# The experts' second bias, moved from the expert units into the routing stage

## The reference, cut to what matters

```python
top_logit, top_idx = lax.top_k(logits, TOP_K)
gates = jax.nn.softmax(top_logit, axis=-1)
...
hu = xblk @ w1[e] + b1[e]
act = x_glu * jax.nn.sigmoid(SWIGLU_ALPHA * x_glu) * (x_lin + 1.0)
return act @ w2[e] + b2[e]
...
y = zeros.at[row_tok].add(yb * row_gate[:, None])
h_lat = h_lat + g2[:, None] * y
```

## Time and profile before

| | us |
|---|---|
| median of 3 runs | 2738.23 (2736.86 to 2741.65) |
| the profiled execution, from its first to its last instruction | 2736.2 |
| TensorE busy | 2587.9 (95%) |
| VectorE busy | 2045.3 (75%) |
| ScalarE busy | 1453.7 (53%) |
| GpSimd busy | 539.6 (20%) |

### The profile page before, as it was taken

One profiled execution on the slowest core, in us unless ns is written; L12 is line 12 of the kernel. 1 busy time (PEld: TensorE's weight loads), 2 busy tenths in 40 slices (PEclk: granted clock), 3 DMA queues, 4 the chain that ended last, 5 costly groups with the idle time before them and its releaser, 6 DMA issues.

```text
span 2736.2 us, 46067 instructions
## 1 busy us (share of the span) xinstructions
PE 2587.9 (95%) x16405; PEld 2212.7 (81%) x16406; DVE 2045.3 (75%) x2500; ACT 1453.7 (53%) x1639; POOL 539.6 (20%) x423
## 2 busy tenths in 40 slices
PE   7998987999896999999999999999999999999995
PEld 3896866777885888777887979899989897898885
DVE  5447888545765987999879787866686778978786
ACT  5446565214443765777557465544454546645554
POOL 0035565200023112121212111110121112111111
PEclk9999998999998999999999999999999999999998
DMA  7121011442333996999879697866586779968783
GB/s 289 39 88 44 22 42 57 173 152 93 109 92 127 386 364 229 365 360 359 287 260 362 235 313 258 283 208 209 190 301 206 247 249 314 344 209 296 261 309 133
DMA packets 274722, 606.26 MB, mean 222 GB/s; under 512 B 21788, under 2 KB 52932, under 8 KB 273520
## 3 DMA queue, kind: packets, MB, share of 16 engines
q1 hardware_dynamic: 254256, 561.62, 57.1%
q0 software_dynamic: 20384, 43.51, 6.9%
HBM read 582.09 MB, written 46.97 MB: 230 GB/s over the span
## 4 chain that ended last, share of the span: by engine, by line
PE 40%; issue 10%; DVE 8%; ACT 4%; DMA 4%; DVEq 1%; POOL 1%; ACTq 0%; POOLq 0%
PE e_acc L2488 7%; PE e_acc L2491 7%; PE e_acc L2489 7%; PE e_acc L2461 5%; PE e_acc L2463 5%; PE e_acc L2462 5%; DMA list_now<-lists 3%; DVE e_slot_r L2646 3%; ACT whi L2574 3%; PE e_tb L2430 1%; DVE yo L2733 1%; DVE e_glu L2709 1%; PE e_acc L2523 1%; DVE e_xlo L2655 1%; POOL sum L2388 1%
## 5 line engine op out<-in xcount | busy, mean ns | idle before, releaser
L2574 ACT ACTIVATE whi<-e_slot 128x2048 fp32r<-128x2048 f32 x296 | 561.0, 1913 | 393.7 <-PE e_acc L2491 327.0
L2646 DVE TENSOR_TENSOR e_slot_r<-e_slot,whi 128x2048 fp32r<-128x2048 f32 x296 | 674.6, 2286 | 106.3 <-ACT whi L2574 106.3
L2488 PE MATMUL e_acc<-e_xhi,whi 128*128 128x256 f32 x1664 | 398.8, 282 | 3.3 <-ACT e_xhi L2578 3.3
L2574 ACT ACTIVATE whi<-slot 128x2048 fp32r<-128x2048 f32 x148 | 283.2, 1913 | 192.4 <-PE e_acc L2463 192.4
L2646 DVE TENSOR_TENSOR slot_r<-slot,whi 128x2048 fp32r<-128x2048 f32 x151 | 344.7, 2285 | 18.1 <-ACT whi L2574 16.5
L2461 PE MATMUL e_acc<-whi,e_ahi 128*128 128x512 f32 x800 | 319.4, 399 | 0.0
L2488 PEld LDWEIGHTS e_acc<-e_xhi,whi 128*128 128x128 f32 x1664 | 313.1, 188 | 6.3 <-ACT e_xhi L2578 6.3
L2463 PE MATMUL e_acc<-whi,e_alo 128*128 128x512 f32 x800 | 313.4, 392 | 0.0
L2462 PE MATMUL e_acc<-e_slot_r,e_ahi 128*128 128x512 f32 x800 | 311.5, 389 | 0.0
L2388 POOL DMA_INDIRECT sum<-yo,e_idx_now x48 | 117.8, 2454 | 973.3 <-issue 518.9
L2461 PE MATMUL e_acc<-whi,e_xhi 128*128 128x512 f32 x768 | 303.6, 395 | 1.8 <-DVE e_slot_r L2646 1.6
(11 more groups left out here) (432 smaller groups left out, 5014.9 us busy)
## 6 DMA issues: line engine op xcount, KB each, us to landing
e_slot<-in_w SPq DMA_DIRECT2D x296, 1024.0 KB, 7.1
slot<-in_w SPq DMA_DIRECT2D x151, 1024.0 KB, 6.4
rv<-in_w_ada SPq DMA_DIRECT2D x32, 512.0 KB, 5.6
slot<-in_w_in SPq DMA_DIRECT2D x9, 1024.0 KB, 9.6
wa<-in_w_ada SPq DMA_DIRECT2D x8, 1024.0 KB, 17.1
slot<-in_w_in SPq DMA_DIRECT2D x12, 512.0 KB, 4.2
xt<-in_x SPq DMA_DIRECT2D x8, 512.0 KB, 14.7
slot<-in_w_out SPq DMA_DIRECT2D x4, 1024.0 KB, 13.9
```

Of the source, the lines that this page charges most:

```text
L2488: pe.matmul(out[:, c, :], whi[i % RING][:, w], xhi[:, kk, :], start=first, stop=False, skip_group_check=True)
L2574: act.activation(whi[i % RING][:], raw[i % PIECES][:], ACT.Copy).then_inc(S["whi_made"], 1)
L2646: v.tensor_tensor(wlo[i % PIECES][:], raw[i % PIECES][:], whi[i % RING][:].bitcast(F32), ALU.subtract).then_inc(S["wlo_made"], 1)
```

## The change

The sum of gate times b2 is formed once per tile in `route` and added to the rows that are stored to `sum`. In `experts` the products with `pick2` and its copy go, and the first product of `down(8)` starts the accumulation.

In `route`, the b2 rows are loaded four times (32 rows each) into one tile, multiplied by g2 and split into high and low (`b2rows`). Per tile VectorE spreads the gates over the 32 experts, four times side by side (`gates_by_expert`), TensorE turns them (`turn_gates`), ScalarE and VectorE split them (`high_gates`, `low_gates`), TensorE multiplies them with `b2rows`, one product per half (`shared_rows`), and VectorE adds the halves to the residual rows, in place (`add_shared`). The store of a tile to `sum` moves behind that. The residual stays in the x tiles, now five; `hot` and `pick` are kept for two tiles and one tile instead of eight. The load of `b1rows` moves behind the load of the first weight pieces, and the last three tiles' shared rows come after it.

```diff
-        XS = 4
+        XS = 5
...
             for i in range(2, XS):
                 load(i)
+            for i in range(4):
+                sp.dma_start(vv[0][i * NE:(i + 1) * NE, :], dram["b2"][0]).then_inc(S["b2_in"], 16)
+            sp.dma_start(vv[1][:], dram["ada_rows"][:, 3 * D:].to_broadcast((P, D))).then_inc(S["b2_in"], 16)
...
             for i in range(LT):
-                sp.wait_ge(S["h_ready"], i + 1)
-                sp.dma_start(dram["sum"][i * P:(i + 1) * P, :], h_[i % 2][:]).then_inc(sum_out[i % 2], 16)
...
                 sp.wait_ge(S["v_ready"], i + 1)
                 sp.dma_start(dram["v_rows"][i * P:(i + 1) * P, :], vv[i % 2][:]).then_inc(v_out[i % 2], 16)
+                if 2 <= i < LT - 1:
+                    store_sum(i - 2)
+                    if i - 2 + XS < LT:
+                        load(i - 2 + XS)
             sp.wait_ge(S["y_done"], LT + 1)
             for i in range(SLOTS):
                 load_piece(sp, dram, keep, raw[i], i, slice(0, 1))
+            sp.wait_ge(S["h_ready"], LT)
+            sp.dma_start(b1rows, ...).then_inc(S["b1_in"], 16)
+            for i in range(LT - 3, LT):
+                store_sum(i)
...
+            def turn_gates(i):
+                pe.wait_ge(S["gates_ready"], i + 1)
+                pe.wait_ge(S["sum_ready"], i)
+                pe.transpose(pg, gates4[i % 2][:].rearrange("p g e -> p (g e)"), ident[:]).then_inc(S["gates_turned"], 1)
+
+            def shared_rows(i, n):
+                if n == 0:
+                    pe.wait_ge(S["gates_low"], 2 * i + 2)
...
+                pe.wait_ge(S["sum_part"], i)
+                pe.wait_ge(S["sum_ready"], i)
+                if n == 1:
+                    pe.wait_ge(S["sum_part"], i + 1)
+                pe.matmul(pb[:], gT[i % 2][:], b2rows[:, n * 512:(n + 1) * 512], start=True, stop=True).then_inc(S["shared_done"], 1)
...
             tt.then_inc(S["b1_turned"], 1)
+            shared_rows(LT - 3, 1)
+            turn_gates(LT - 2)
+            shared_rows(LT - 2, 0)
+            shared_rows(LT - 2, 1)
+            turn_gates(LT - 1)
+            shared_rows(LT - 1, 0)
+            shared_rows(LT - 1, 1)
...
+            act.wait_ge(S["b2_scaled"], 1)
+            act.activation(b2rows[:], vv[0][:], ACT.Copy).then_inc(S["b2_high"], 1)
+
+            def high_gates(i):
+                act.wait_ge(S["gates_turned"], i + 1)
+                act.wait_ge(S["shared_done"], 2 * max(0, i - 1))
+                act.activation(gT[i % 2][:], pg, ACT.Copy).then_inc(S["gates_high"], 1)
...
             exponents(LT - 1)
+            high_gates(LT - 2)
+            high_gates(LT - 1)
             act.wait_ge(S["y_done"], LT + 1)
...
+            def gates_by_expert(i):
+                v.wait_ge(S["pairs_ready"], i + 1)
+                c.link(v.tensor_tensor(gated[:], hot[i % 2][:], pairs[:, i, :, 1].unsqueeze(2).to_broadcast((P, TOPK, NE)), ALU.mult))
+                c.link(v.tensor_reduce(gate_of[:], gated[:].rearrange("p k e -> p e k"), AX.X, ALU.add))
...
+                v.tensor_copy(gates4[i % 2][:], gate_of[:].unsqueeze(1).to_broadcast((P, 4, NE))).then_inc(S["gates_ready"], 1)
+
+            def low_gates(i):
+                v.wait_ge(S["gates_high"], i + 1)
+                for at in (NE, 3 * NE):
+                    v.tensor_tensor(gT[i % 2][at:at + NE], pg[at:at + NE], gT[i % 2][at:at + NE].bitcast(F32), ALU.subtract).then_inc(S["gates_low"], 1)
+
+            def add_shared(i, n):
+                at = slice(n * 512, (n + 1) * 512)
+                v.wait_ge(S["shared_done"], 2 * i + n + 1)
...
+                v.tensor_tensor(x[i % XS][:, at], pb[:], x[i % XS][:, at], ALU.add).then_inc(S["sum_ready" if n else "sum_part"], 1)
...
                 if j == 0:
                     low_rows(0)
+            v.wait_ge(S["b2_in"], 16 * 5)
+            v.tensor_tensor(vv[0][:], vv[0][:], vv[1][:], ALU.mult).then_inc(S["b2_scaled"], 1)
+            v.wait_ge(S["b2_high"], 1)
+            v.wait_ge(S["b2_scaled"], 1)
+            v.tensor_tensor(b2rows[2 * NE:], vv[0][2 * NE:], b2rows[2 * NE:].bitcast(F32), ALU.subtract).then_inc(S["b2_ready"], 1)
             v.wait_ge(S["const_in"], 16 * NCONST)
...
                 if i:
                     residual(i - 1)
+                if i >= 3:
+                    low_gates(i - 3)
                 if i >= 2:
                     choose(i - 2)
                 if i + 1 < LT:
                     low_rows(i + 1)
+                if i >= 3:
+                    add_shared(i - 3, 0)
                 if i:
                     normed(i - 1)
                 if i >= 2:
                     targets(i - 2)
+                    gates_by_expert(i - 2)
+                if i >= 3:
+                    add_shared(i - 3, 1)
...
             v.wait_ge(S["units_done"], 2)
-            v.wait_ge(S["bias_ready"], 2)
+            for i in (LT - 2, LT - 1):
+                gates_by_expert(i)
+            for n in range(2):
+                add_shared(LT - 3, n)
+            for i in (LT - 2, LT - 1):
+                low_gates(i)
+                for n in range(2):
+                    add_shared(i, n)
+            v.wait_ge(S["bias_ready"], 1)
             v.wait_ge(S["b1_turned"], 1)
...
-                                if i == 8:
-                                    pe.matmul(out[:, b, :], pick2[:], bias[:, j * 512:(j + 1) * 512], start=True, stop=False)
...
-                    pe.wait_ge(S["pick_ready"], u * 2 + 2)
+                    pe.wait_ge(S["pick_ready"], u + 1)
...
-                v.tensor_copy(pick2[2 * NE:], own[2 * NE:, bass.ds(u, 1)].to_broadcast((2 * NE, P))).then_inc(S["pick_ready"], 1)
```

More of the change, by code:

```diff
@@ L1771, in route @@
         mlo = [t.sb(f"o_mlo{j}", [P, KT, P], F32R) for j in range(2)]
-        h_ = [t.sb(f"o_h{j}", [P, D]) for j in range(2)]
+        part = t.sb("o_part", [P, D])
         sq = t.sb("o_sq", [P, D])
@@ L1786, in route @@
         pairs = t.sb("o_pairs", [P, LT, TOPK, 2])
-        hot = t.sb("o_hot", [P, LT, TOPK, NE])
-        pick = t.sb("o_pick", [P, LT, TOPK, NE])
+        hot = [t.sb(f"o_hot{j}", [P, TOPK, NE]) for j in range(2)]
+        pick = t.sb("o_pick", [P, TOPK, NE])
+        gated = t.sb("o_gated", [P, TOPK, NE])
+        gate_of = t.sb("o_gate_of", [P, NE])
+        gates4 = [t.sb(f"o_gates4{j}", [P, 4, NE]) for j in range(2)]
+        gT = [t.sb(f"o_gT{j}", [P, P], F32R) for j in range(2)]
+        b2rows = t.sb("o_b2rows", [P, D], F32R)
         sel = t.sb("o_sel", [P, LT, NE])
@@ L1873, in project_out @@
                 for k in range(KT):
+                    if k in (2, 6) and i >= 3:
+                        shared_rows(i - 3, k // 4)
                     if k == KT // 2 and i >= 2:
@@ L1891, in project_last @@
                     for k in range(KT):
+                        if k == KT // 2:
+                            shared_rows(i - 3, n)
                         if (n, k) == (1, 0):
@@ L2007, in _ @@
                     turned_rows(i - 1)
+            high_gates(LT - 3)
             root(LT - 1)
@@ L2080, in targets @@
                 c.link(v.tensor_tensor(place[:, i, :], pp[:, i * NE:(i + 1) * NE], base[:], ALU.add))
-                c.link(v.tensor_tensor(pick[:, i], hot[:, i], place[:, i, :].unsqueeze(1).to_broadcast((P, TOPK, NE)), ALU.mult))
-                c.link(v.tensor_reduce(dest[:, four], pick[:, i], AX.X, ALU.add))
+                c.link(v.tensor_tensor(pick[:], hot[i % 2][:], place[:, i, :].unsqueeze(1).to_broadcast((P, TOPK, NE)), ALU.mult))
+                c.link(v.tensor_reduce(dest[:, four], pick[:], AX.X, ALU.add))
                 v.tensor_copy(desti[:, four], dest[:, four]).then_inc(S["dest_ready"], 1)
@@ L2125, in _ @@
             targets(LT - 2)
+            low_gates(LT - 3)
             choose(LT - 1)
@@ L2205, in shared @@
     keep["bias"] = top("bias", [P, 2 * D], F32R)
-    keep["pick"] = [top(f"pick{i}", [P, P], F32R) for i in (1, 2)]
+    keep["pick"] = top("pick", [P, P], F32R)
     keep["top"] = at
@@ L2458, in turn_act, with three @@
                         turn(lin[:, 0, :], 0, g % 2).then_inc(S["turned"], TURN_STEP[nb][g])
-                    def three(out, hi, lo, k, c, wh, wl, last):
-                        pe.matmul(out, hi[:, k, c], wh, start=False, stop=False)
+                    def three(out, hi, lo, k, c, wh, wl, last, first=False):
+                        pe.matmul(out, hi[:, k, c], wh, start=first, stop=False)
                         pe.matmul(out, hi[:, k, c], wl, start=False, stop=False)
@@ L2526, in down @@
                                     kk = 2 * (i - 8) + k
-                                    mm = three(out[:, b, :], ahi, alo, kk, slice(b * P, (b + 1) * P), whi[i % RING][:, w], wlo[i][:, w], kk == KT - 1)
+                                    mm = three(out[:, b, :], ahi, alo, kk, slice(b * P, (b + 1) * P), whi[i % RING][:, w], wlo[i][:, w], kk == KT - 1, kk == 0)
                             if j == 0 and between:
```

77 lines of the change are left out of this document (47 added, 30 removed).

## The result

The changed kernel takes 2749.59 us (median of 8 runs, 2742.33 to 2751.5), the kernel before 2737.9 in the same comparison (8 runs, 2732.91 to 2741.65): ratio 1.0039, interval 1.003 to 1.0048. That is 10.7 us more by the ratio; the medians are 11.7 apart. Predicted were 2740, range 2732 to 2748. The stages are read from one profiled execution of each kernel. That of the changed kernel took 2751.47 us, nearly the longest of its eight.

A forecast was written before the change was run, and what follows sets the result against it. TensorE was taken to bound large units and routing's tiles, VectorE small units. Terms -18.4 + 3.7 + 2.4 + 4.3 + 0.9 + 8.9 = +1.8 us gave a span of 2738.0, median about 2740, range 2732 to 2748.

The forecast's parts named there:

- The units: Experts' units: removed products save 12.0 us in large units, the dropped pick copy 6.0 in small ones; sum -18.4 us.
- C: Rival, faster: TensorE sets the small units, so 23 us goes, and the clock does not drop; 2733 us, chance 0.13.
- D: Rival: the removed products in the units were hidden and nothing goes; 2758 us, chance 0.02.
- These are queued behind a fifth x tile: Routing's start: b2 copies and gate row load behind an x tile, landing at 731.9 us, signal about 732.2.
- 3.7 us at turn 2: Routing's start: turn_merged(2) moves from 734.99 to about 738.7 us as VectorE waits for b2's loads; +3.7, bounds 3 and 5.
- The clock: Routing's start: after TensorE's 3.5 us pause it runs at 1.2 GHz for a while; +2.4 us, bounds 0 and 3.4.
- The tiles: Routing's tiles: ten added products and five gate transposes on TensorE, +4.3 us; VectorE's added work hidden; last tile +0.9.
- rival B: Slower: VectorE becomes the bound of routing's tiles, +5 us; 2745 us, chance 0.07.
- the worked-through tile: Routing: VectorE's steps in one tile end at 14.7 us, the next projection at 16.2, leaving 1.5 to spare.
- its extra chain of 0.9: Last routing tile: one product per half and ScalarE's high_gates ahead of root make it 0.9 us later, bounds 0.5 and 1.5.
- The end: Routing's end: b1's late landing, then a chain of products and additions across engines; +8.9 us, bounds 7 and 13.
- Rival A: Slower: handovers behind b1's landing make routing's end 13 us late, and its start pause reaches its bounds; 2746 us, chance 0.2.

The follow-up runs named there:

- e1: The kernel before without the units' b2 products and second pick copy, nothing put into routing (b2 missing from the output): 2719.66 us, ratio 0.9942.
- e3: The changed kernel with the four b2 loads and the gate row's load issued ahead of the router's weights, scaling left in place: 2741.51 us, ratio 1.0022.
- e12: e11 with 187 instructions of satisfied waits on TensorE, moving its loop over the units in the code without a branch: 2734.61 us, ratio 0.9993.
- e6: The kernel before with 35 never-executed products behind a branch, moving TensorE's loop over the units 72 instructions later: 2744.5 us, ratio 1.0028.
- e10: The changed kernel with VectorE's first subtraction of the experts' stage waiting until GpSimd has made both first gathers: 2743.98 us, ratio 1.0033.
- e7: The changed kernel with two small VectorE copies ahead of the first unit's pick, to start its subtractions later: 2747.97 us, ratio 1.0036.
- e2: The changed kernel with b2's scaling and split moved behind tile 0's residual and tile 2's low rows, loads unmoved: 2738.27 us, ratio 1.0007.
- e8: The changed kernel with b1 loaded earlier and the last shared products on free PSUM banks between the unit table's steps: 2738.75 us, ratio 1.0006.
- e4: The changed kernel with GpSimd's clearing of stale semaphores moved to the end of the experts' stage: 2749.51 us, ratio 1.0056.
- e11: The changed kernel with the edits of e2, e8 and e10 together: 2724.66 us, ratio 0.9955.

## Why the prediction was wrong

**The units: right.** -18.4 was said; e1 has -18.7 for units 1 to 36, and the changed kernel -17.1 without unit 4. TensorE's 0.23 us per product in large units and the pick in VectorE's unbroken row in small ones are borne out, so rivals C and D were rightly small.

No single step carries the miss. One term of the sum was mis-sized by much, and two costs were put at nothing.

**The failed step: "These are queued behind a fifth x tile", the landing at 732.2.** The product on b2 was to start there; it started at 738.95, 6.7 us later, of which 2.3 came from before routing. So 3.7 us at turn 2 became 8.1, and 6 to 11 over the seven profiles. Counted from the stage's first load, the row was forecast at 18.6 us and landed at 21.3 to 24.4. I divided the bytes in the queue by 353 GB/s and left out the two b1 loads issued right behind, which are under way beside the row. Their 0.52 MB are 1.5 us at that rate, an estimate. And the rate did not hold: 310 GB/s in 727.5 to 735.0 and 248 in 735.0 to 738.3, with DMA shares of 1.01 and 0.98. e3, with the same bytes earlier, takes 5.5 us back; how much of it is the b1 loads and how much the rate is argued, not shown. The operations' own chain was sized right: 6.5 us from product to turn, predicted and measured (738.95 to 745.41). The clock cost 1.6 instead of 2.4 (up to 2.4 in the other six).

**Two costs were put at nothing.** The larger is unit 4's stall, 4.5 us against e12's and e1's 40.3 to 40.4 (2.9 to 4.5 in the nine kernels of the new routing that have it), by 73 instructions of code put in ahead of the loop (e6 makes it in the old kernel, e12 removes it in the new one). The other is the first gather, 1.8 us: without the second pick it ends behind both of VectorE's subtractions instead of the first (e1 has it without any change to routing, e10 removes it). That VectorE's head start, 0.37 us larger by the dropped copy, is the reason was my guess, and e7 speaks against it: it gave the time back, and the gather still waited for both. Together the two are 6.3 of the 11.5 us by which the sum was short.

**The tiles: right in kind, too dear.** VectorE kept a wait of 1.80 us in each tile, so rival B was wrong and the worked-through tile right; a tile with two shared products and a turn of gates takes 16.18 us instead of 15.61, so products with several waits cost nearly their bare 0.23. The last tile took 1.0 more, so of its extra chain of 0.9 some 0.4 appeared. 2.8 instead of 5.2.

**The end: right mechanism, 1.6 short.** The chain ended 24.9 us after the last logits, as predicted (875.9 in the old clock is 24.8), by luck, two errors that cancel: it began 1.0 earlier, and product and addition took 1.67 instead of 1.4. Short were SyncE's last store, 3.3 us from issue to passing instead of 2.6, and the meeting of the engines behind it, 1.0 us, which I left out. Rival A names this relay, but its point, routing over 24 us longer, was not reached: 23.0 without what came before.

Of the 11.5 us between the forecast sum and the measured one, 3.6 are the start, 1.6 the end, 4.5 unit 4, 1.8 the gather and 2.3 scatter before routing; the tiles gave 2.4 back.

## What to carry to other kernels

A load is priced by when its row lands among everything under way on the same engines, with a range of some us for it, not by bytes over the best rate; and work that waits for it does not stand ahead of a row the tensor engine needs (e2: one move, 8.8 us). A relay between two engines over one PSUM bank costs its whole chain, here 1.67 us a link, so work appended at a stage's end is put on free banks between steps that already wait (e8: 9 us). And where the sum nearly cancels, look also at what merely shifts: an engine's code, and what runs beside a gather at the next stage's head. A stage is read in more than one execution before a few us of it are explained.

## What the runs showed of the hardware

**Code.** TensorE idled 3.0 to 3.4 us at the first small unit behind a large one in nine kernels (the changed one, e2 to e4 and e7 to e11) and in e6, with a 16 KB transfer on the instruction queue just ahead, and was granted a clock of 0.50 for 3.4 to 6.8 us from around its end on. It is a matter of the first passes: in the changed kernel the last such transfer began at 1098.8 us, and the loop ran 32 more times without one. The Trainium skill, "Runtime: NRT & Kernel Launch", Instruction fetch mechanics, says code comes in 16 KiB blocks of 256 instructions and a taken branch to a block not held must wait for its transfer. That would explain e6: the loop was moved by 72 instructions, 0.28 of a block. The trace agrees in the size of the transfer and in the stall at a branch; which block it was, no run shows.

**Gathers.** An indirect gather's instruction took 1.0 to 1.1 us where no 128x2048 subtraction of VectorE ended in it. All others, 73 or 74 of the 74 gathers in each of the fourteen profiles, ended 0.87 to 0.97 us after the end of such a subtraction. The Trainium skill, "SBUF — State Buffer", SBUF: two separate sides, has VectorE and GpSimd share a port that one instruction holds to its end, for a subtraction with two SBUF inputs only against GpSimd work that reads SBUF. The rows agree if the gather's reading of its index column is such work; that was not tried by itself.

**Waits.** Satisfied waits on TensorE's queue seem not to be free: 140 instructions of them lengthened a stretch in which TensorE had 7 us of idle time by 7.9 us (e12 against e11). A transfer of code at 871.0 lies in that stretch too, and no run separates it.
